# The last token tile of an SSD and attention layer written apart, its first tile's loads reordered, and merge weights asked for one unit earlier

## The chip, the core and the metric

The kernel runs on 1 core of a Trainium2 chip. TensorE (PE) multiplies, VectorE (DVE), ScalarE (ACT) and GpSimd (POOL) do the elementwise work, SyncE (SP) and ScalarE issue the DMAs. The metric is the device time of one execution in microseconds, the median of a few runs.

## The reference, cut to what matters

```python
h = rms_norm(x, norm_gain)                       # x: (1, 1024 tokens, 1024), all float32
q, k, v, z_a, z_s, xbc, dt_raw, gate_pre = split(h @ w_in)
branch_a = (window_attention(q, k, v, ...) * silu(z_a)) @ w_attn_proj
# SSD: causal conv + silu of xbc -> xs (32 heads of 64), B and C (4 groups of 128 states)
w = (C @ B.T) * decay * dt                       # inside a chunk
y = w @ xs + exp(a_cs) * (C @ prev_state) + d_skip * xs
state = state * chunk_decay + B.T @ (decay_to_end * dt * xs)   # handed to the next chunk
branch_b = rms_norm(y * silu(z_s), ssd_norm_gain) @ w_ssd_proj
merged = sigmoid(g_A) * branch_a + sigmoid(g_B) * branch_b
out = x + merged @ w_out
```

The state that a chunk leaves is read by the next chunk only. No one reads what the last one leaves.

## The kernel before, in words

Every float32 product is made exact enough by splitting both operands in a high and a low part and multiplying three of the four pairs, so each product of a weight unit (1024 x 128) with 512 tokens takes 24 matmuls of 128x512. ScalarE writes the high part of a weight unit (`high`, L189), GpSimd the low part (`low`, L192), and the raw unit comes by `load_w` (L199 to L205) into one of two slots; unit u may be loaded when the low part of unit u-2 is done. Unit u is multiplied when its low part is done.

The program has three blocks, one behind the other on each engine.

Block 1 (0 to 490 us) makes q, k, v, the conv channels and a part of z, and stores them to DRAM. Its last pair of units leaves `raw` in the tile `acc`, which is stored to `z_d`.

Block 2 (L1062 to L1488) walks over 8 tiles of 128 tokens in a loop. In each tile PE has eight halves of weight units to multiply (`half_unit(0)` to `half_unit(7)`, four units of gates and z), and between them the small products of attention and SSD: transposes (L1136), scores (L1129), attention times v (L1150), C times B (L1160), the inner part of y (`diag`, L1166), the part from the state (`off`, L1173) and the new state (`new_state`, L1179). SP loads a tile's operands in a fixed order in `tile_loads` (L1078): q, k, v, xb (16 rows of conv channels), then bc (B and C), a weight unit, `csb` (32 rows of cumulated decays, broadcast to 128 partitions: 2 MB), `zo`, `ecsb` (two broadcasts to 64 partitions each) and three more weight units. In the first tile bc goes ahead of the weight unit and of csb. csb, ecsb and yo (the output of the SSD) share the tile `acc` with what block 1 leaves there.

Block 3 has three passes of 8 weight units: the attention projection (unit 0 to 7, `unit3`, its operand o in X1), the first half of the SSD projection (8 to 15, operand in X0), the second half (16 to 23) with the merge, and then the output projection (24 to 31). Its units are called w0 to w31 here. Ahead of pass one the 8 tiles of o are loaded back from DRAM (L1552, L1554) and split, the first two tiles by DVE (L1713, L1716), six by ACT and DVE (L1661, L1716). PE's unit w2 needs `low` of w2, which GpSimd does after the squares of the first y tile (L1629, L1631). Those wait for ACT's sigmoid of the first gate tile (L1665) and the silu of the first y tile (L1653, L1703), and the loads of these wait on SP for the last stores of block 2. In the merge (L1729 to L1743) ACT does per unit the sigmoid of a gate, the high part of the merged half 0, `high` of the weight two units on, and the high part of half 1; DVE finishes a unit with the low part of half 1 (`m_lo`), and SP waits for that before it goes on to the next weight.

## Time and profile before

| | us |
|---|---|
| median of 3 runs (lowest, highest) | 1408.21 (1408.12, 1411.24) |
| the profiled execution | 1405.1 |
| its span | 1403.3 |
| PE busy in the span | 1356.0 |
| DVE, ACT, POOL busy | 794.6, 612.2, 586.9 |
| block 1, block 2, block 3 on PE | 0 to 490, 493 to 1026, 1026 to 1398 |

The span is what the trace covers; 1.8 us of the execution lie around it. The granted clock of PE is at its upper level in nearly the whole span (mean 0.99). Busy time alone doesn't show what is lost: the few places where PE stands still are read in its timeline, and what it waits for in the timelines of the other engines.

### The profile page before, as it was taken

What the parts mean: (1) busy time and instruction counts of PE and PEld (TensorE: products, weight loads), DVE (VectorE), ACT (ScalarE), POOL (GpSimd) and SP (SyncE); (2) the same over time, 40 slices, a digit from 0 to 9 for tenths busy, and PEclk for the clock granted to TensorE, in tenths of its full rate; (3) what the DMA queues carried; (4) which work ended last, traced back from release to release, by engine and by line L of the source; (5) the groups of instructions that cost most, each with busy time, mean ns of one, the idle gap of its engine ahead of it and who ended that gap; (6) DMA issues with size and microseconds to landing.
All of it is one profiled execution on the core that took longest, in us unless ns stands there. A gap on an engine that the chain in (4) does not pass through costs nothing.

```text
span 1403.3 us, 20569 instructions
## 1 busy us (share of the span) xinstructions
PE 1356.0 (97%) x7108; PEld 1085.9 (77%) x7108; DVE 794.6 (57%) x955; ACT 612.2 (44%) x1148; POOL 586.9 (42%) x344
## 2 busy tenths in 40 slices
PE   4999999999999989999999999999999999999999
PEld 4877777888888767778787878878768888777787
DVE  5876777766776344755565564646365554555311
ACT  5654435544455352525253545444356633323110
POOL 3634555544455342333333234243337666443321
PEclk9999999999999989999999999999999999999999
DMA  8333453433222475778777686767486265334421
GB/s 221 143 98 105 150 166 105 174 111 120 92 103 105 147 162 163 177 202 158 201 164 199 171 214 152 229 145 203 139 290 237 105 220 195 138 132 168 149 105 60
DMA packets 173669, 221.61 MB, mean 158 GB/s; under 512 B 7760, under 2 KB 136016, under 8 KB 173376
## 3 DMA queue, kind: packets, MB, share of 16 engines
q1 hardware_dynamic: 137808, 172.64, 43.3%
q10 hardware_dynamic: 35728, 48.37, 9.5%
q8 instruction: 19, 0.31, 0.1%
q14 instruction: 18, 0.15, 0.0%
q0 software_dynamic: 96, 0.13, 0.0%
HBM read 152.57 MB, written 63.31 MB: 154 GB/s over the span
## 4 chain that ended last, share of the span: by engine, by line
PE 79%; issue 9%; DVE 5%; DMA 3%; POOL 3%; ACT 2%; ACTq 0%; SPq 0%; POOLq 0%; DVEq 0%
PE F L180 34%; PE F L960 27%; PE F L1818 3%; PE M L1818 3%; PE M L1136 2%; PE M L1179 2%; DMA sb_early<-x_d 2%; POOL sb_res L1642 1%; PE F L1173 1%; PE F L1166 1%; PE F L1150 1%; PE M L1173 1%; PE M L1166 1%; PE F L1771 1%; DMA sb_early<-x 1%
## 5 line engine op out<-in xcount | busy, mean ns | idle before, releaser
L180 PE MATMUL F<-sb_xb,sb_whl 128*128 128x512 f32 x1536 | 376.7, 402 | 0.0
L180 PEld LDWEIGHTS F<-sb_xb,sb_whl 128*128 128x128 f32 x1536 | 287.1, 189 | 75.2 <-issue 8.8
L192 POOL TENSOR_TENSOR sb_whl<-sb_wst,sb_whl 128x1024 fp32r<-128x1024 f32 x64 | 160.7, 2511 | 403.6 <-ACT sb_whl L189 403.1
L180 PE MATMUL F<-sb_X,sb_whl 128*128 128x512 f32 x1104 | 259.5, 396 | 3.6 <-POOL sb_whl L192 2.6
L180 PEld LDWEIGHTS F<-sb_X,sb_whl 128*128 128x128 f32 x1104 | 206.6, 187 | 56.0 <-issue 5.5
L960 PE MATMUL F<-sb_tv,sb_whl 128*128 128x512 f32 x1008 | 243.5, 397 | 2.3 <-DVE sb_acc L761 2.3
L960 PEld LDWEIGHTS F<-sb_tv,sb_whl 128*128 128x128 f32 x1008 | 190.0, 189 | 49.4 <-issue 2.7
L415 POOL TENSOR_TENSOR sb_whl<-sb_acc,sb_whl 128x512 fp32r<-128x512 f32 x103 | 146.1, 1426 | 137.6 <-ACT sb_whl L472 137.6
L960 PE MATMUL F<-sb_xb,sb_whl 128*128 128x512 f32 x756 | 186.4, 399 | 1.8 <-DVE sb_part L751 1.8
L960 PEld LDWEIGHTS F<-sb_xb,sb_whl 128*128 128x128 f32 x756 | 142.2, 189 | 40.3 <-issue 5.0
L189 ACT ACTIVATE sb_whl<-sb_wst 128x1024 fp32r<-128x1024 f32 x64 | 67.6, 1057 | 208.3 <-DMA sb_wst<-w_units 108.3
L1406 ACT ACTIVATE sb_res<-F 128x512 f32<-128x512 f32 x64 | 38.3, 598 | 182.0 <-PE F L180 182.0
L807 DVE SCALAR_TENSOR_TENSOR M<-sb_acc,M 128x1023 f32<-128x1023 f32 (+2 forms) x72 | 92.4, 1284 | 15.7 <-ACT M L574 14.8
L472 ACT ACTIVATE sb_whl<-sb_acc 128x512 fp32r<-128x512 f32 x103 | 63.7, 627 | 73.0 <-PE F L960 61.6
L415 POOL TENSOR_TENSOR sb_whl<-sb_wst,sb_whl 128x512 fp32r<-128x512 f32 x44 | 63.9, 1454 | 75.4 <-ACT sb_whl L472 75.3
L1397 ACT ACTIVATE sb_early<-sb_acc,sb_ncs_sb 128x128 f32<-128x128 f32 x256 | 77.4, 394 | 7.5 <-DVE sb_acc L1292 7.5
L1301 DVE TENSOR_TENSOR sb_early<-sb_early 128x1024 f32<-128x1024 f32 x32 | 45.9, 1454 | 55.5 <-ACT sb_early L1397 55.5
L1706 DVE SCALAR_TENSOR_TENSOR sb_X<-sb_X,sb_cst x16 | 54.6, 3411 | 35.9 <-POOL sb_part L1629 35.9
L1306 DVE TENSOR_TENSOR sb_acc<-sb_acc,M 128x512 f32<-128x512 f32 x16 | 11.0, 688 | 79.6 <-PE M L1173 72.8
L1465 POOL TENSOR_TENSOR sb_early<-sb_early,sb_ssd_sb 128x512 f32<-128x512 f32 x32 | 32.8, 1046 | 49.5 <-DVE sb_early L1276 49.5
L1703 DVE TENSOR_TENSOR sb_X<-sb_X x16 | 23.0, 1441 | 51.4 <-ACT sb_X L1653 51.4
L1629 POOL TENSOR_TENSOR sb_part<-sb_X 128x1024 f32 x16 | 30.3, 1896 | 46.0 <-DVE sb_X L1703 46.0
(223 smaller groups left out, 1780.3 us busy)
## 6 DMA issues: line engine op xcount, KB each, us to landing
sb_wst<-w_units SPq DMA_DIRECT2D x64, 512.0 KB, 6.1
sb_acc<-cs_d SPq DMA_DIRECT2D x8, 2048.0 KB, 21.6
sb_wst<-w_units SPq DMA_DIRECT2D x12, 1024.0 KB, 4.9
x_d<-sb_res ACTq DMA_DIRECT2D x24, 512.0 KB, 2.6
sb_acc<-w_units SPq DMA_DIRECT2D x10, 1024.0 KB, 5.0
sb_early<-x_d SPq DMA_DIRECT2D x8, 1024.0 KB, 9.1
sb_acc<-ecs_d SPq DMA_DIRECT2D x16, 512.0 KB, 23.4
z_d<-sb_res ACTq DMA_DIRECT2D x16, 512.0 KB, 6.6
```

The lines of the kernel that those rows point to most:

```text
L180: last = nc.tensor.matmul(bank, weight(slot, wp, k), act(ap, k, half), start=(k == 0 and wp == 0 and ap == 0), stop=(k == NK - 1 and wp == 1))
L189: return nc.scalar.activation(weights(slot, 0), raw_unit(slot), ACT.Copy)
L192: return nc.gpsimd.tensor_tensor(weights(slot, 1), raw_unit(slot), weights(slot, 0).bitcast(f32), ALU.subtract)
L415: nc.gpsimd.tensor_tensor(ring(idx, 1), operand(n, order(n)[idx]), ring(idx, 0).bitcast(f32), ALU.subtract).then_inc(p_lo, 1)
L472: nc.scalar.activation(ring(idx, 0), operand(n, order(n)[idx]), ACT.Copy).then_inc(p_hi, 1)
L807: ins = nc.vector.scalar_tensor_tensor(to[:, back:], raw[:, u, 0:T - back], tap(2 * m + u, 3 - back), to[:, back:], ALU.mult, ALU.add)
L960: last = nc.tensor.matmul(F[:, BANK[what], :], ring(idx, wp)[:, k * P:(k + 1) * P], moving(what, ap, k), start=(idx < 4 and k == 0 and wp ...
L1301: nc.vector.tensor_tensor(dec[:, g % 2], dec[:, g % 2], cbm[:, g, :].unsqueeze(1).to_broadcast([P, HG, P]), ALU.mult).then_inc(wT_ready, 1)
L1397: last = nc.scalar.activation(dec[:, g % 2, h, :], csb[:, HG * g + h, :], ACT.Exp, bias=ncs_sb[:, ds(j, 1), HG * g + h:HG * g + h + 1].rea ...
L1406: nc.scalar.activation(res[:, p, (h % 2) * HALF:(h % 2 + 1) * HALF], F2[:, h % 2, :], ACT.Copy).then_inc(half_taken, 1)
L1706: nc.vector.scalar_tensor_tensor(split_tile(X, 1, i, s), y, C("ssd_gain", q0, q0 + 8)[:, ds(i * 2 + s, 1)], tile(X, 0, i, s), ALU.mult, AL ...
L1818: last = nc.tensor.matmul(row_bank(t), X0[:, ap, k, t * P:(t + 1) * P], w_half[wp][:, (k % 2) * HALF:(k % 2 + 1) * HALF], start=(k == 0 an ...
```

## The change

Five things, which go together in the text of the program:

- Block 2's loop runs over 7 tiles, and the last tile is written apart, without the transposes of B, the products and sums of the new state, the decay of the old state and their waits.
- In that last tile ACT takes the high parts of all eight o tiles as soon as PE is done with `off(3)`, ahead of `take_half(7)` and `unit_out(3)`; POOL makes the low parts of o tiles 3 and 5, DVE those of the other six. DVE makes no high parts any more. The store of y is issued before the last unit is taken, not after.
- First tile: SP issues q, k, v, xb first, then w0 and w1 of this block, then csb, bc and the next weight unit. The waits for the stores of `z_d` move from ahead of csb to ahead of zo, and GpSimd waits for them before its loop.
- In the tile `acc` csb moves to the upper end, so that ecsb and yo lie over `raw`.
- Merge: w18 and w19 are asked for ahead of the loop, and in the loop w(20 + 2i + s) is asked for where w(19 + 2i + s) was, ahead of the load of the residual rows.

```diff
+    def loop_and_last(self, eng_loop, count, steps):
+        for i in self.loop(eng_loop, count - 1, steps):
+            yield i, False
+        yield count - 1, True
...
-            sp.wait_ge(p_lo, 7 * NPAIR)
-            load_w(sp, 0, 0, 0)
-            load_w(sp, 1, 0, 0)
...
-        csb, w = carve(acc_all, 0, NHS, P)
-        ecsb, w = carve(acc_all, w, 16, P)
+        ecsb, w = carve(acc_all, 0, 16, P)
         yo, w = carve(acc_all, w, 16, P)
+        csb, w = carve(acc_all, w, NHS, P)
...
+        O_POOL = (3, 5)
+        O_DVE = NK - len(O_POOL)
...
                 if first:
+                    sp.wait_ge(p_lo, 7 * NPAIR)
+                    load_w(sp, 0, 0, 0)
+                    load_w(sp, 1, 0, 0)
+                    load_decays(j, at_j)
                     sp.wait_ge(prod, 7 * (NPAIR - 1) + 5)
                     load_bc(j, at_j)
-                load_w(sp, B2 + 2, 4, j)
-                sp.wait_ge(dec_ready, j * 4 + 1)
+                    load_w(sp, B2 + 2, 4, j)
+                else:
+                    load_w(sp, B2 + 2, 4, j)
+                    load_decays(j, at_j)
+                    load_bc(j, at_j)
+                sp.wait_ge(o_stored, j * 16 + 16)
                 if first:
                     for p in range(2):
                         sp.wait_ge(z_stored[p], 16 * 4)
-                sp.dma_start(csb[:], cs_d[:, ds(at_j, P)].partition_broadcast(P)).then_inc(cs_in, 16)
-                if not first:
-                    load_bc(j, at_j)
-                sp.wait_ge(o_stored, j * 16 + 16)
...
-                new_state(0)
-                new_state(1)
+                if not last_tile:
+                    pe.wait_ge(brow_ready, at(1, 1))
+                    new_state(0)
+                    new_state(1)
...
                 take_half(6)
-                take_half(7)
-                unit_out(3)
+                if last_tile:
+                    act.wait_ge(yg_done, 4 * NT + 1)
+                    for k in range(NK):
+                        act.wait_ge(o_in[k], 16)
+                        nc.scalar.activation(X1[:, 0, k, :], X1[:, 1, k, :].bitcast(f32), ACT.Copy).then_inc(o_hi, 1)
+                else:
+                    take_half(7)
+                    unit_out(3)
                 act.wait_ge(yout_ready, at(4, 5))
                 act.dma_start(y_d[:, :, ds(j * P, P)].rearrange("n p t -> p n t"), yo[:]).then_inc(y_stored, 16)
+                if last_tile:
+                    take_half(7)
+                    unit_out(3)
...
+                if last_tile:
+                    for k in O_POOL:
+                        pool.wait_ge(o_hi, k + 1)
+                        nc.gpsimd.tensor_tensor(X1[:, 1, k, :], X1[:, 1, k, :].bitcast(f32), X1[:, 0, k, :].bitcast(f32),
+                                                ALU.subtract).then_inc(o_lo, 1)
...
+            load_w(sp, B3 + 18, 0, 0)
+            load_w(sp, B3 + 19, 0, 0)
             with nc.sync.Fori(0, 3) as i:
                 for s in range(2):
-                    load_w(sp, B3 + 18 + s, 2, i)
                     sp.wait_ge(m_lo, i * 4 + (2 * s + 2))
                     load_merge(i + 1, s)
+                    load_w(sp, B3 + 20 + s, 2, i)
                     load_rows(i, s)
-            for s in range(2):
-                load_w(sp, B3 + 24 + s, 0, 0)
...
             for k in range(NK):
-                if k < DVE_TILES:
-                    dve.wait_ge(o_in[k], 16)
-                    ch.link(nc.vector.tensor_copy(X1[:, 0, k, :], X1[:, 1, k, :].bitcast(f32)))
-                else:
-                    dve.wait_ge(act_hi, k - DVE_TILES + 1)
-                nc.vector.tensor_tensor(X1[:, 1, k, :], X1[:, 1, k, :].bitcast(f32), X1[:, 0, k, :].bitcast(f32),
-                                        ALU.subtract).then_inc(act_lo, 1)
+                if k not in O_POOL:
+                    dve.wait_ge(o_hi, k + 1)
+                    nc.vector.tensor_tensor(X1[:, 1, k, :], X1[:, 1, k, :].bitcast(f32), X1[:, 0, k, :].bitcast(f32),
+                                            ALU.subtract).then_inc(act_lo, 1)
```

SP's issues at the start of block 2, first tile, before. `sb_early<-x_d` with 16 rows is xb, with 8 rows bc; `sb_acc<-cs_d` is csb, `sb_acc<-ecs_d` ecsb, `sb_wst<-w_units` a weight unit.

```order
L205 DMA sb_wst<-w_units 128x1024
L1062 UNCONDITIONAL_BRANCH
L1080 DMA sb_early<-q_d 128x8x128
L1081 DMA sb_early<-k_d 128x2x192
L1084 DMA sb_early<-v_d 128x256
L1087 DMA sb_early<-x_d 128x16x128
L1076 DMA sb_early<-x_d 128x8x128
L205 DMA sb_wst<-w_units 128x1024
L1096 DMA sb_acc<-cs_d 128x32x128
L1100 DMA sb_early<-z_d 128x8x128
L1103 DMA sb_acc<-ecs_d 64x16x128
```

The same piece now:

```order
L1077 UNCONDITIONAL_BRANCH
L1099 DMA sb_early<-q_d 128x8x128
L1100 DMA sb_early<-k_d 128x2x192
L1103 DMA sb_early<-v_d 128x256
L1106 DMA sb_early<-x_d 128x16x128
L211 DMA sb_wst<-w_units 128x1024
L1091 DMA sb_acc<-cs_d 128x32x128
L1095 DMA sb_early<-x_d 128x8x128
L1123 DMA sb_early<-z_d 128x8x128
L1126 DMA sb_acc<-ecs_d 64x16x128
```

The first two weight units moved behind xb, and csb moved ahead of bc (a weight unit still stands between bc and z_d).

PE at the end of the last tile, before: the last halves of units (L180), diag (L1166), off (L1173), new_state (L1179), and the first product of block 3 (L1771).

```order
L1166 MATMUL M<-sb_early 64x128 x8
L1173 MATMUL F<-sb_early,sb_part 128x128 x4
L1173 MATMUL M<-sb_early,sb_part 128x128 x4
L1179 MATMUL M<-sb_early 128x512 x2
L180 MATMUL F<-sb_xb,sb_whl 128x512 x24
L1755 UNCONDITIONAL_BRANCH
L1771 MATMUL F<-sb_X,sb_whl 128x512 x24
```

And now:

```order
L1190 MATMUL M<-sb_early 64x128 x8
L1197 MATMUL F<-sb_early,sb_part 128x128 x4
L1197 MATMUL M<-sb_early,sb_part 128x128 x4
L186 MATMUL F<-sb_xb,sb_whl 128x512 x24
L1792 UNCONDITIONAL_BRANCH
L1811 MATMUL F<-sb_X,sb_whl 128x512 x24
```

`new_state` is gone between off and the last half of a unit.

## Rows read from the trace of the kernel before

**Rows 1.** The page, part 4: the chain that ended last, shares by engine

```profile
PE 79%; issue 9%; DVE 5%; DMA 3%; POOL 3%; ACT 2%; ACTq 0%; SPq 0%; POOLq 0%; DVEq 0%
```

**Rows 2.** Chain of waits, first pass of block 3: start us, us, what

```profile
1038.25 84.00 PE F L180 x360
```

**Rows 3.** Timeline of PE, merge: start us, us, line, operands, xcount [idle <-releaser]

```profile
1213.00 45.36 PE L180 MATMUL F<-sb_X,sb_whl 128*128 128x512 f32 x192
1259.86 23.02 PE L180 MATMUL F<-sb_X,sb_whl 128*128 128x512 f32 x96 [1.50 <-POOL sb_whl L192]
...
1315.83 5.85 PE L1818 MATMUL F<-sb_whl,sb_X 128*128 128x512 f32 x24 [0.90 <-DVEq L1736]
```

**Rows 4.** Timelines of SP and ACT, merge: a weight's load and high part

```profile
1249.67 0.33 SPq L205 DMA_DIRECT2D sb_wst<-w_units  x1
...
1256.10 1.06 ACT L189 ACTIVATE sb_whl<-sb_wst 128x1024 fp32r<-128x1024 f32 x1 [4.01 <-DMA sb_wst<-w_units]
```

**Rows 5.** Timelines of POOL and DVE, merge: two instructions at one time

```profile
1228.89 2.41 POOL L192 TENSOR_TENSOR sb_whl<-sb_wst,sb_whl 128x1024 fp32r<-128x1024 f32 x1 [3.36 <-ACT sb_whl L189]
...
1229.47 2.38 DVE L1738 TENSOR_TENSOR sb_acc<-sb_acc,sb_res 128x512 f32 x1
```

**Rows 6.** Timeline of PE, last tile and first product of block 3

```profile
1018.77 1.88 PE L1179 MATMUL M<-sb_early 128*128 128x512 f32 x4
1020.09 6.15 PE L180 MATMUL F<-sb_xb,sb_whl 128*128 128x512 f32 x24
...
1031.40 6.85 PE L1771 MATMUL F<-sb_X,sb_whl 128*128 128x512 f32 x18 [2.80 <-DVE sb_X L1716]
```

**Rows 7.** Timelines of SP, ACT, DVE and POOL from the last tile into block 3

```profile
1014.83 3.36 SPq L1552 DMA_DIRECT2D sb_X<-o_d  x7
1023.88 0.34 SPq L1554 DMA_DIRECT2D sb_X<-o_d  x1
...
1027.56 0.48 ACTq L1449 DMA_DIRECT2D y_d<-sb_acc  x1
1028.58 5.79 ACT L1661 ACTIVATE sb_X<-sb_X 128x1024 fp32r<-128x1024 f32 x6 [0.75 <-issue]
1038.54 1.28 ACT L1665 ACT_TABLE_LOAD   x1 [4.17 <-DMA sb_acc<-g_d]
...
1029.67 7.36 DVE L1716 TENSOR_TENSOR sb_X<-sb_X 128x1024 fp32r<-128x1024 f32 x6 [2.08 <-ACT sb_X L1661]
...
1049.65 3.19 POOL L192 TENSOR_TENSOR sb_whl<-sb_wst,sb_whl 128x1024 fp32r<-128x1024 f32 x1 [0.16 <-POOL sb_ssd_sb L1631]
```

**Rows 8.** L1554's instruction, landing times

```profile
DMA to landing us min/median/max: 3.7/3.7/3.7
```

**Rows 9.** Timeline of PE, first tile of block 2

```profile
493.15 1.18 PE L1136 MATMUL M<-sb_cst,sb_early 128*128 128x128 f32 x8 [3.52 <-issue]
...
508.96 1.47 PE L1136 MATMUL M<-sb_cst,sb_early 128*128 128x128 f32 x12
...
522.38 1.97 PE L1136 MATMUL M<-sb_cst,sb_early 128*128 128x128 f32 x8 [4.44 <-DVE sb_early L1287]
524.00 7.70 PE L180 MATMUL F<-sb_xb,sb_whl 128*128 128x512 f32 x24
```

**Rows 10.** Windows of 4 us: PE, PEld, DVE, ACT, POOL busy, PEclk, DMA share, GB/s

```profile
524.00:528.00 4.00, 4.00 (x12) 3.14 (x11) 0.84 (x2) 3.12 (x10) 0.00 (x0) 0.50 0.48 36
```

**Rows 11.** Timelines of SP, DVE and ACT, first and second tile

```profile
484.64 0.38 SPq L1087 DMA_DIRECT2D sb_early<-x_d  x1
...
552.69 0.38 SPq L1087 DMA_DIRECT2D sb_early<-x_d  x1
...
518.32 2.36 DVE L1292 TENSOR_TENSOR sb_acc<-sb_acc,sb_ssd_sb 128x1024 f32<-128x1024 f32 x2 [10.84 <-DMA sb_acc<-cs_d]
...
546.00 1.06 ACT L189 ACTIVATE sb_whl<-sb_wst 128x1024 fp32r<-128x1024 f32 x1 [13.67 <-DMA sb_wst<-w_units]
```

**Rows 12.** Chain of waits, second tile: the load of bc

```profile
561.65 22.83 DMA sb_early<-x_d
```

More of the change, by code:

```diff
@@ L1059, in build, with tiles @@
             "q_in", "k_in", "x2_in", "v_in", "bc_in", "cs_in", "ecs_in", "z_in", "o_stored", "y_stored")
+        def tiles(loop):
+            with loop(0, NT - 1) as j:
+                yield j, False
+            yield NT - 1, True
+        o_in = sems(*[f"o_in{k}" for k in range(NK)])
+        o_hi, o_lo = sems("o_hi", "o_lo")
+        O_POOL = (3, 5)
+        O_DVE = NK - len(O_POOL)
         @block.sync
@@ L1117, in _ @@
             pe.wait_ge(b12_moved, 32)
-            with nc.tensor.Fori(0, NT) as j:
+            for j, last_tile in tiles(nc.tensor.Fori):
                 def at(n, k):
@@ L1237, in _ @@
                 off(3)
-                pe.wait_ge(state_ready, at(4, 3))
-                new_state(2)
-                new_state(3)
+                if not last_tile:
+                    pe.wait_ge(state_ready, at(4, 3))
+                    new_state(2)
+                    new_state(3)
                 half_unit(7)
@@ L1248, in _ @@
             ch.link(nc.vector.tensor_scalar(stat[:, 5, :], C("sinks"), -1.0, None, ALU.mult))
-            for j in ch.loop(nc.vector.Fori, NT, 4 * 3 + 2 * 2):
+            for j, last_tile in ch.loop_and_last(nc.vector.Fori, NT, 4 * 3 + 2 * 2):
                 def at(n, k):
@@ L1350, in _ @@
                 y_take(0)
-                add_state(0)
-                add_state(1)
+                if not last_tile:
+                    add_state(0)
+                    add_state(1)
                 weights_T(2)
@@ L1371, in _ @@
             act.wait_ge(ncs_ready, 1)
-            with nc.scalar.Fori(0, NT) as j:
+            for j, last_tile in tiles(nc.scalar.Fori):
                 def at(n, k):
@@ L1425, in _ @@
                 probs_out(1)
-                act.wait_ge(brt_done, at(1, 1))
-                nc.scalar.activation(flat(brow[:]), S[:, 0, :], ACT.Copy).then_inc(brow_ready, 1)
+                if not last_tile:
+                    act.wait_ge(brt_done, at(1, 1))
+                    nc.scalar.activation(flat(brow[:]), S[:, 0, :], ACT.Copy).then_inc(brow_ready, 1)
                 unit_out(0)
@@ L1455, in _ @@
             pool.wait_ge(state_zero, 1)
-            with nc.gpsimd.Fori(0, NT) as j:
+            for p in range(2):
+                pool.wait_ge(z_stored[p], 16 * 4)
+            for j, last_tile in tiles(nc.gpsimd.Fori):
                 def at(n, k):
@@ L1499, in build @@
             "ms_done", "ms_rt", "rms_ready", "acc_ready", "m_hi", "m_lo", "rows_in", "row_done", "out_ready", "out_stored")
-        o_in = sems(*[f"o_in{k}" for k in range(NK)])
         gateA_in = sems("gateA_in0", "gateA_in1")
@@ L1656, in silu_and_high @@
                                      scale=C("ssd_gain", q0, q0 + 8)[:, ds(i * 2 + s, 1)]).then_inc(act_hi, 1)
-            act.wait_ge(st_done, 4 * NT)
-            for k in range(DVE_TILES, NK):
-                act.wait_ge(o_in[k], 16)
-                nc.scalar.activation(X1[:, 0, k, :], X1[:, 1, k, :].bitcast(f32), ACT.Copy).then_inc(act_hi, 1)
             with nc.scalar.Fori(0, 4) as i:
@@ L1768, in unit3 @@
                         for k in range(NK):
-                            pe.wait_ge(act_lo, tiles + k + 1)
+                            if tiles == 0 and k in O_POOL:
+                                pe.wait_ge(o_lo, O_POOL.index(k) + 1)
+                            else:
+                                pe.wait_ge(act_lo, tiles + k + 1 - (0 if tiles else sum(q < k for q in O_POOL)))
                             for wp, ap in ((0, 0), (0, 1), (1, 0)):
@@ L1783, in _ @@
                     unit3(2 + s, X1, i)
-            unit3(8, X0, 0, tiles=8)
+            unit3(8, X0, 0, tiles=O_DVE)
             unit3(9, X0, 0)
```

45 lines of the change are left out of this document (25 added, 20 removed).

## The prediction, made before the changed kernel was run

> **What bounds the kernel now.** I read the page first. Its chain of waits lies on PE for 79% of the span, and what it calls issue is mostly time around PE's small steps [rows 1]. So an edit pays only where PE stands still, or where it takes work off PE. The next view is PE's timeline, which marks each stretch of matmuls and the idle time ahead of it. PE is late in three places: in the first tile of block 2, between block 2 and block 3, and in the merge. The change touches all three. The timelines of the other engines, read backwards from each idle time, tell what was late. A matmul of 128x512 costs 84.00 / 360 = 0.2333 us when nothing waits [rows 2]: 24 of them 5.60 us, a unit of 48 11.20 us.
>
> **The merge: -7.5 us.** Units 16 to 23 are 384 matmuls, and 24 of the output projection follow before the last stretch shown. From 1213.00 to 1315.83 are 102.83 us, and 408 x 0.2333 is 95.2, so 7.6 us are lost, with the slow first matmul of the last stretch 7.9 [rows 3]. The releaser of the first wait is GpSimd's low part of a weight. Its high part on ACT waited 4.01 us for the DMA, which was asked for at 1249.67 and had landed by 1256.10, 6.4 us later [rows 4]. The loop closes on itself: SP asks for a weight only behind the wait for `m_lo` of the unit before, ACT stands in that wait with the high part of half 1 queued behind it, and that high part gives the next `m_lo`. The period of this loop is longer than PE's 11.2 us, so PE meets it from the third unit on.
>
> Now w20 is asked for when w19 was, one unit of 11.2 us further on. The load of 6.4 us is hidden by PE's own unit, and `high` of a weight then waits for PE to be done with the slot two units back, which leaves 11.2 - 1.06 - 2.41 = 7.7 us of slack for the two splits [rows 4, 5]. The x rows go behind the weight on SP's queue. They are needed in the output projection alone. w19 itself waits for the low part of w17 and stands ahead of the second merge load only by that, long before PE needs it. Nothing else in the loop has a period of more than a unit as far as I see. Bounds: 2.4 (the 1.50 and the 0.90 that the shown rows mark as waits, were another chain almost as long) to 7.9. I take 7.5, near the upper end, because the slack is so large.
>
> **The last tile and the start of block 3: -2.5 us.** Off PE go two stretches of `new_state`, each 1.88 us as shown and 1.7 without the overlap at its end, and 4 of the 12 transposes of a row of 1.47, or 0.5 [rows 6, 9]. Together that is 3.9 us. The last `half_unit` started at 1020.7 and ended at 1026.3; now it should end at 1022.4. The first product with o ended at 1038.25, which is where the long stretch begins [rows 2]. So PE took 12.0 us for 5.6 us of work: it waited for the low parts of o (2.80 in the last wait), and 18 matmuls took 6.85 us in place of 4.2 [rows 6].
>
> Who makes the parts now: the loads of o start when the store of o lands, 1014.83 before, now 2.2 earlier (one new_state and the transposes are gone ahead of it), 1012.6. DVE is free of y when the load of the last o tile is issued, 1023.88 before. That moves by the same 2.2 and by two state sums less on DVE, about 1.3, to 1020.4, and the tile lands 3.7 us later, 1024.1 [rows 7, 8]. ACT's copies cost 5.79 / 6 = 0.97 each and can start when `off(3)` is done, 1016.8; the eighth ends near 1025.5. DVE's low parts cost 7.36 / 6 = 1.23 each from 1020.4 on, GpSimd's two 2.4 each. If they run side by side, the first product ends near 1029.5, 8.8 earlier than before.
>
> What is late next: unit w2. PE would ask for it one half and one unit after that, 1029.5 + 16.8 = 1046.3. Its low part ended at 1052.84, and PE asked at 1038.25 + 16.8 = 1055.05. The chain to this low part starts at the store of y: issued 1027.56, the first gate tile lands and ACT starts on it at 1038.54, and another 14.3 us of table load, sigmoid, silu, product, squares and low part end at 1052.84 [rows 7]. None of it is shortened by the change. The store of y now stands directly behind the eighth copy, so it is issued near 1026 in place of 1027.56, and the store of the last unit goes behind it, which holds SP's wait for both. So w2 is ready near 1051.3. PE then stands still for about 5 us. A pause like that has a second price: after 4.44 us of idle time in the first tile PE's granted clock was 0.50 for 4 us (1.2 GHz in place of 2.4), and the next 24 matmuls took 7.70 in place of 5.60, 2.1 more [rows 9, 10]. Gain: 1055.05 - 1051.3 - 2.1 = 1.7. If the pause is shorter because the low parts of o come later, PE's pauses are the same ones in another place. The old pauses had the same price, though, and I give back part of it: 2.5. Bounds: -1 (w2 ready 1 us earlier only, and a clock price of 2.1) to 8.8 (w2 is no limit).
>
> VectorE and GpSimd beside each other are a doubt of its own. While GpSimd ran a low part from 1228.89 to 1231.30, a sum of 128x512 on DVE that had started at 1229.47 ended at 1231.85, after it [rows 5]. So the two seem not to run their two-input instructions at once. In the change six DVE and two GpSimd subtractions stand for PE together: 6 x 1.23 + 2 x 2.4 = 12.2 us from 1020.4 on if in turn, so the first product ends near 1033.3 and PE asks for w2 at 1050.1. That is just under 1051.3, so the gain changes by little. The Trainium skill, "SBUF — State Buffer", Terms, says the port pair of VectorE and GpSimd is locked for a whole instruction and the loser blocks. By that rule giving tiles 3 and 5 to GpSimd gains nothing over leaving them on DVE (12.2 against 8 x 1.23 = 9.8); the row agrees with the lock.
>
> **The first tile: 0 us.** Before, csb landed at 518.3 and DVE had waited 10.84 us for it; PE lost 4.44 us and the clock's 2.1 [rows 9, 11]. Now csb is asked for some 11 us earlier, behind xb and two weights. But bc is behind csb now, and PE needs bc at its transposes, which were reached at 508.96 [rows 9]. The second tile has the same order of loads: xb was issued at 552.69 and bc landed at 561.65 + 22.83 = 584.48, 31.8 us later [rows 11, 12]. From 484.64, with one weight more in front, that gives 516.5 to 518. PE would reach the transposes near 507.7, as xb lands 1 to 2 us sooner without the 1 MB of weights ahead of it. So PE waits 9 to 10 us there, and pays the clock's 2.1, where it had waited 4.44 and 2.1 later on and 3.52 ahead of its first matmul, of which it saves 1.3. csb then no longer costs it anything. Balance: +9.5 - 4.4 - 1.3 = +3.8 at that place. Behind it PE had to wait anyway: the fourth weight unit landed at 546.0, behind all of the tile's loads, and the decays, the state and `diag(2)` hung on it [rows 11]. The sum of the bytes ahead of it is the same, the two weights at the front start 2 us later, and 1 us of a hole ahead of csb closes. This end moves by less than 2 us either way, and it swallows most of the 3.8. I take 0. Bounds: -2 (bc lands at 513, the rest follows it) to +5 (bc at 520 and the PE bound).
>
> Moved at no cost: GpSimd's wait for `z_d` stands ahead of a loop whose first instruction waits for DVE anyway. The new place of csb holds no other reader. The tiles 1 to 6 have the same instructions in the same order. More instructions are fetched, since the last tile is written apart; no wait for code of more than a us shows at the block changes.
>
> **Sum.** 0 - 2.5 - 7.5 = -10.0 us on the profiled execution: span 1393.3, execution 1395.1. The median of the runs stands 3.1 us above the profiled execution, so 1408.2 - 10.0 = 1398.2.
>
> **The rivals.**
> - A. The start of block 3 is free (8.8 in place of 2.5). For it: the chain to w2 has 2.2 us of slack now, and y is stored earlier. Against: its 25 us don't get shorter. 1391.9. Chance 0.10.
> - B. bc holds the first tile in full and the clock price stays: first tile +5, start of block 3 nearer to its lower end, 0. 1408.2 + 5 - 7.5 = 1405.7. For it: the second tile's loads. Against: the weight at 546.0 gives room. Chance 0.12.
> - C. The merge doesn't get what it says: another step of its loop (the merge loads behind `m_lo`, GpSimd's product) is as long, and only 2.4 come. 1403.3. Against: the wait named is the DMA's. Chance 0.08.
> - D. Slower than before: csb's descriptors, started among the xb and z traffic, go at a much lower rate, and bc with them. It decides if bc lands later than about 529: then the first tile costs over 12 us, more than the rest gains. At 535 (18 us behind the forecast's 517) it is 1398.2 + 18 = 1416. Against: the second tile had the same mixture and took 31.8 us. Chance 0.04.
> - The forecast has 0.66.
>
> **How the numbers follow.** A run of this kernel can be told from no change from about 0.3%, 4.2 us. Faster (below 1404.0): the forecast, A, and most of C, with a rest of the forecast's own spread taken off, 0.84. Same: B and the near ends, 0.11. Slower: D and a corner of B, 0.05. The range reaches to A on one side and past C on the other: 1391 to 1404. The forecast's own range is 1394 to 1402.
>
> **What would show it.** In the merge ACT's high parts wait for no DMA, and PE runs from unit 16 into the output projection with no idle time over 0.5 us; the stretch is about 95 us. At the start of block 3 the first product ends 4 to 9 us after the last `half_unit`'s 5.6, and PE has a new idle time ahead of w2, with GpSimd's low part as its releaser and the clock at its lower level behind it. In the first tile PE's idle time ahead of L1136 at 522 is gone, and one of 7 to 10 us ahead of the transposes of bc, released by the DMA, is there. I am wrong if PE waits for the merge's weights still, if w2 shows no wait, or if bc lands before 512 or after 522.

## The result, and the profile after

| | before | changed |
|---|---|---|
| median, us (lowest, highest; runs) | 1408.62 (1408.12, 1411.24; 4) | 1394.70 (1390.57, 1399.94; 4) |
| the profiled execution, its span | 1405.1, 1403.3 | 1399.9, 1398.1 |

The ratio is 0.990 (95% interval 0.986 to 0.994), 13.9 us between the medians where 10.0 were forecast. The four runs lie 9.4 us apart, and the profiled one is the slowest of them, so its span is only 5.2 us shorter than before's. It shows what each part did, but not how much is given back on average. For that the experiments below leave twelve more profiles.

**The first tile.** PE's timeline; names and columns as in [rows 9], `transpose` is L1159 now and a unit's half L186:

```profile
489.30 1.09 PE L1159 MATMUL M<-sb_cst,sb_early 128*128 128x128 f32 x8
...
494.77 11.46 PE L186 MATMUL F<-sb_xb,sb_whl 128*128 128x512 f32 x48 [2.47 <-POOL sb_whl L198]
...
507.39 0.65 PE L1159 MATMUL M<-sb_cst,sb_early 128*128 128x128 f32 x4 [0.28 <-DMA sb_early<-x_d]
...
515.48 1.09 PE L1159 MATMUL M<-sb_cst,sb_early 128*128 128x128 f32 x8
516.33 5.83 PE L186 MATMUL F<-sb_xb,sb_whl 128*128 128x512 f32 x24
```

The wait of 4.44 us and the slow 24 matmuls behind it are gone, and PE waits 0.28 us for bc where 9 to 10 were expected. The tile starts 3.9 us earlier, and the second one (its first scores) at 558.81 in place of 569.59: 10.8 us, where 0 was forecast. SP's timeline shows how; `x_d` is xb and then bc, `cs_d` is csb:

```profile
475.33 0.37 SPq L1099 DMA_DIRECT2D sb_early<-q_d  x1
...
477.43 0.38 SPq L1106 DMA_DIRECT2D sb_early<-x_d  x1
480.10 1.45 SPq L211 DMA_DIRECT2D sb_wst<-w_units  x2
481.59 0.43 SPq L1091 DMA_DIRECT2D sb_acc<-cs_d  x1
483.60 10.98 SPq L1095 DMA_DIRECT2D sb_early<-x_d  x1
494.68 5.38 SPq L211 DMA_DIRECT2D sb_wst<-w_units  x1
505.30 0.37 SPq L1123 DMA_DIRECT2D sb_early<-z_d  x1
```

And the same of before, with SP's longest wait there:

```profile
482.37 0.38 SPq L1080 DMA_DIRECT2D sb_early<-q_d  x1
...
485.12 4.34 SPq L1076 DMA_DIRECT2D sb_early<-x_d  x1
495.06 0.34 SPq L205 DMA_DIRECT2D sb_wst<-w_units  x1
497.05 0.39 SPq L1096 DMA_DIRECT2D sb_acc<-cs_d  x1
```

```profile
SPq L205 <- POOL sb_whl L415: 36.8, 1, 36.8
```

The reader is to see two things. xb was issued at 484.64 [rows 11] only because it stood behind w0, and w0 waits for GpSimd's last low part of block 1; now it goes at 477.43. And csb went at 497.05, behind the third weight (495.06) and the end of z_d's stores; now it goes at 481.59, 15.5 us earlier, while the last two stores of z_d are still to be issued (487.99 and 490.59); over its old room it could not. The fourth weight lands 10.8 us earlier with them, 535.2 for 546.0.

**Given back.** In the profiled run the later tiles lose 8.3 of the 10.8 us: the last one starts at 959.32 where it was 961.84. Three of PE's waits in block 2:

```profile
575.98 1.11 PE L1159 MATMUL M<-sb_cst,sb_early 128*128 128x128 f32 x4 [2.93 <-DMA sb_early<-x_d]
...
578.45 7.43 PE L186 MATMUL F<-sb_xb,sb_whl 128*128 128x512 f32 x24
...
841.72 0.65 PE L1159 MATMUL M<-sb_cst,sb_early 128*128 128x128 f32 x4 [1.64 <-DMA sb_early<-x_d]
...
908.12 0.65 PE L1159 MATMUL M<-sb_cst,sb_early 128*128 128x128 f32 x4 [0.96 <-DMA sb_early<-x_d]
```

These are waits for bc, 5.5 us in all, which lands 22.6 us after its issue in the median and 25.0 at most (before 21.4 and 22.8). Behind the first of them PE also runs slowly, 7.43 us for 24 matmuls. This is the most that any profile gives back; the mean over all of them is 0.7 us, as the paragraph on all profiles below says. In the chain of waits DMA has 9% in place of 3% [rows 1]:

```profile
PE 76%; DMA 9%; issue 6%; DVE 4%; POOL 3%; ACT 2%; SPq 0%; ACTq 0%; POOLq 0%; DVEq 0%
```

**The last tile and block 3.** PE, answering to [rows 6]:

```profile
1014.15 5.84 PE L186 MATMUL F<-sb_xb,sb_whl 128*128 128x512 f32 x24
...
1027.74 2.93 PE L1811 MATMUL F<-sb_X,sb_whl 128*128 128x512 f32 x6 [0.71 <-POOL sb_X L1531]
1032.13 1.65 PE L1811 MATMUL F<-sb_X,sb_whl 128*128 128x512 f32 x3 [1.47 <-DVE sb_X L1753]
1033.58 18.02 PE L186 MATMUL F<-sb_X,sb_whl 128*128 128x512 f32 x72
1052.65 67.45 PE L186 MATMUL F<-sb_X,sb_whl 128*128 128x512 f32 x288 [1.05 <-POOL sb_whl L198]
```

The new wait ahead of w2 is there, behind GpSimd's low part, but it is 1.05 us long, where the forecast had 5 or, with the low parts in turn, 1.2, and the clock does not fall behind it (288 matmuls in 67.45 us, 0.234 each). w2 starts 2.4 us earlier than before (1055.05), and block 2 had already brought 2.5: the part itself gave nothing in this run. ACT shows why. Its first copy of an o tile, here and in a second run of almost the same kernel (E12 below):

```profile
1016.34 1.06 ACT L1479 ACTIVATE sb_X<-sb_X 128x1024 fp32r<-128x1024 f32 x1 [5.19 <-DMA sb_X<-o_d]
```

```profile
1008.88 2.17 ACT L1479 ACTIVATE sb_X<-sb_X 128x1024 fp32r<-128x1024 f32 x2 [3.28 <-PE M L1197]
```

Counted from the start of the last tile, E12's copy starts at 55.0 us, released by `off(3)` as the forecast has it. This one starts at 57.0, released by the load of o. The store of y stands behind the copies, so here it is issued 66.7 us into the tile, later than before (65.7), and in E12 at 64.1. DVE and GpSimd beside each other, the low parts of o:

```profile
1023.24 2.22 DVE L1753 TENSOR_TENSOR sb_X<-sb_X 128x1024 fp32r<-128x1024 f32 x1 [1.33 <-ACT sb_X L1479]
1025.79 6.29 DVE L1753 TENSOR_TENSOR sb_X<-sb_X 128x1024 fp32r<-128x1024 f32 x2 [0.33 <-ACT sb_X L1479]
```

```profile
1024.55 3.13 POOL L1531 TENSOR_TENSOR sb_X<-sb_X 128x1024 fp32r<-128x1024 f32 x1 [0.18 <-ACT sb_X L1479]
1028.54 2.46 POOL L198 TENSOR_TENSOR sb_whl<-sb_wst,sb_whl 128x1024 fp32r<-128x1024 f32 x1 [0.85 <-ACT sb_whl L195]
```

Two subtractions that take 1.23 us each alone took 6.29 together beside two instructions of GpSimd.

**The merge.** PE, answering to [rows 3]:

```profile
1210.85 90.16 PE L186 MATMUL F<-sb_X,sb_whl 128*128 128x512 f32 x384
1301.31 5.86 PE L1858 MATMUL M<-sb_whl,sb_X 128*128 128x512 f32 x24 [0.30 <-issue]
1310.67 5.85 PE L1858 MATMUL F<-sb_whl,sb_X 128*128 128x512 f32 x24 [3.51 <-DVEq L1773]
```

The units run through without a wait, as forecast, and then PE stands 3.51 us ahead of the second part of the output projection. It waits there for a pair of PSUM banks that DVE has not taken yet: the merge on ACT, GpSimd and DVE is behind. From the first of these starts to the one after the last shown (1316.36) are 105.5 us, before 108.5: 3.0 gained, not 7.5.

### The profile page after: what moved, and what is told of

It reads as the page before. It is cut to its first block, busy times and chain, and to the rows that moved or that the text cites. A ratio compares the mean times of both kernels' runs of the same rounds, so it can differ in the third digit from the quotient of the medians.

```text
span 1398.1 us, 20354 instructions
## 1 busy us (share of the span) xinstructions
PE 1353.0 (97%) x7096; PEld 1082.6 (77%) x7096; DVE 810.9 (58%) x947; ACT 613.4 (44%) x1148; POOL 582.4 (42%) x338
## 4 chain that ended last, share of the span: by engine, by line
PE 76%; DMA 9%; issue 6%; DVE 4%; POOL 3%; ACT 2%; SPq 0%; ACTq 0%; POOLq 0%; DVEq 0%
PE F L186 32%; PE F L963 27%; DMA sb_early<-x_d 7%; PE F L1858 3%; PE M L1858 3%; PE M L1159 2%; POOL sb_res L1687 1%; PE M L1203 1%; PE F L1197 1%; PE F L1190 1%; PE F L1173 1%; PE M L1197 1%; PE M L1190 1%; POOL sb_whl L198 1%; DMA sb_early<-x 1%
## 5 line engine op out<-in xcount | busy, mean ns | idle before, releaser
L186 PE MATMUL F<-sb_xb,sb_whl 128*128 128x512 f32 x1536 | 376.1, 402 | 2.5 <-POOL sb_whl L198 2.5
L186 PEld LDWEIGHTS F<-sb_xb,sb_whl 128*128 128x128 f32 x1536 | 286.6, 188 | 77.0 <-issue 10.4
L186 PE MATMUL F<-sb_X,sb_whl 128*128 128x512 f32 x1104 | 259.8, 397 | 1.1 <-POOL sb_whl L198 1.1
L186 PEld LDWEIGHTS F<-sb_X,sb_whl 128*128 128x128 f32 x1104 | 207.8, 188 | 52.8 <-issue 1.7
L963 PEld LDWEIGHTS F<-sb_xb,sb_whl 128*128 128x128 f32 x756 | 142.3, 189 | 40.3 <-issue 5.0
L418 POOL TENSOR_TENSOR sb_whl<-sb_wst,sb_whl 128x512 fp32r<-128x512 f32 x44 | 64.1, 1458 | 75.6 <-ACT sb_whl L475 75.6
L1327 DVE TENSOR_TENSOR sb_early<-sb_early 128x1024 f32<-128x1024 f32 x32 | 56.8, 1794 | 52.4 <-ACT sb_early L1425 52.3
L1858 PE MATMUL F<-sb_whl,sb_X 128*128 128x512 f32 x192 | 46.2, 396 | 3.5 <-DVEq L1773 3.5
L1505 POOL TENSOR_TENSOR sb_early<-sb_early,sb_ssd_sb 128x512 f32<-128x512 f32 x28 | 29.6, 1079 | 45.0 <-DVE sb_early L1302 38.0
```

The costliest lines, as they stand in the source:

```text
L186: last = nc.tensor.matmul(bank, weight(slot, wp, k), act(ap, k, half), start=(k == 0 and wp == 0 and ap == 0), stop=(k == NK - 1 and wp == 1))
L418: nc.gpsimd.tensor_tensor(ring(idx, 1), operand(n, order(n)[idx]), ring(idx, 0).bitcast(f32), ALU.subtract).then_inc(p_lo, 1)
L963: last = nc.tensor.matmul(F[:, BANK[what], :], ring(idx, wp)[:, k * P:(k + 1) * P], moving(what, ap, k), start=(idx < 4 and k == 0 and wp ...
L1327: nc.vector.tensor_tensor(dec[:, g % 2], dec[:, g % 2], cbm[:, g, :].unsqueeze(1).to_broadcast([P, HG, P]), ALU.mult).then_inc(wT_ready, 1)
L1858: last = nc.tensor.matmul(row_bank(t), X0[:, ap, k, t * P:(t + 1) * P], w_half[wp][:, (k % 2) * HALF:(k % 2 + 1) * HALF], start=(k == 0 an ...
```

## The experiments

All compare with the kernel before on the same chip. "Merge stretch" is PE's time from the start of unit 16 to the third part of the output projection (before 108.5); "second tile" and "last tile" are the starts of their scores (before 569.6 and 961.8); "boundary" is from the last tile's start to unit 16 (before 251.2).

**E1. The changed kernel once more.** No edit.

> The changed kernel once more, to have a second profile and its spread. Theory T: the first tile gains about 10.8 us (PE's second tile starts near 559 where before started at 569.6), and bc, which waits behind csb, gives back an amount that differs from run to run: the profiled run above, 1399.9, gave back 8.3 us by the last tile, so a run near 1392 should give back almost nothing. Median 1391 to 1398, the runs 5 us or more apart, and in the new profile the waits of PE for bc (DMA from x_d) are fewer or shorter when its time is lower. Rival R: the spread lies elsewhere (the start of block 3 or the merge), and the last tile of block 2 starts 2.5 us earlier than before in any run.

1391.88 us (1390.94 to 1395.54, 6 runs, so 4.6 us apart where 5 or more were expected), ratio 0.990 (0.988 to 0.992). The profile is of a run of 1390.98: second tile 558.9, last tile 951.7, so of 10.7 us 10.1 are still there; PE waits 0.8 us for bc in all tiles together, against 5.8 in the run of 1399.94. T holds in the main: of the 9 us between these two runs 7.6 stand there at the last tile, and 2.6 more come between it and unit 16. The merge stretch was 106.7.

**E2. The merge alone.** On the kernel before:

```diff
+            load_w(sp, B3 + 18, 0, 0)
+            load_w(sp, B3 + 19, 0, 0)
             with nc.sync.Fori(0, 3) as i:
                 for s in range(2):
-                    load_w(sp, B3 + 18 + s, 2, i)
                     sp.wait_ge(m_lo, i * 4 + (2 * s + 2))
                     load_merge(i + 1, s)
+                    load_w(sp, B3 + 20 + s, 2, i)
                     load_rows(i, s)
-            for s in range(2):
-                load_w(sp, B3 + 24 + s, 0, 0)
```

> The kernel before with the merge's weights asked for one unit further on, and nothing else. Theory T: 3.0 us off before, as the two profiles show from 1213 to the output projection (105.5 in place of 108.5 us); PE's idle time ahead of the output projection grows from 0.90 to about 3.5, since another chain of the merge loop (ACT's sigmoid, GpSimd's product, DVE's sums) has a period of about 12.0 us against PE's 11.2. Rival R, the prediction's: 7.5 us, the wait of 3.5 being an accident of one run.

1403.42 us (12 runs) against 1406.87, ratio 0.998 (0.996 to 0.999): 3.2 us (1.3 to 5.2). Merge stretch 106.95, and the wait of 3.47 us is back, with a slow x24 behind it (7.41). T holds, the 7.5 does not. Beside the kernel before's own 108.5 the stretch shows 1.6 us, beside the mean of all profiles of the old form (109.5) 2.6.

**E3. The first tile alone.** The order of the loads, csb at the upper end of `acc` and GpSimd's earlier wait, on the kernel before (these pieces of the diff ahead of the prediction, no others).

> The kernel before with the first tile's loads, the room of csb and GpSimd's earlier wait for z_d changed, and nothing else. Theory T: the second tile starts 10 to 11 us earlier; later tiles give back between 0 and 8 of it at the waits for bc, so the time is 2.5 to 10.8 us under before and its runs are further apart than before's. Rival R, the prediction's: 0 us (between -2 and +5).

1395.68 us (6 runs), ratio 0.992 (0.990 to 0.994): 11.0 us (8.3 to 13.8), just above the upper end of T. Second tile 558.8, last tile 952.3. This one part brings three quarters of the whole, and the forecast gave it nothing. Its runs (1394.6 to 1399.3) are not further apart than before's (1402.0 to 1411.1 in 23), so that half of T's expectation is not shown.

**E4. The last tile alone.** Written apart on the kernel before, with the copies and subtractions of o moved as in the change.

> The kernel before with the last tile written apart, and nothing else. Theory T: 0 to 1 us off before, since unit w2 of block 3 hangs on the store of y and the first gate tile and starts 2.4 us earlier only because all of block 2 did; PE waits about 1 to 4 us ahead of w2. Rival R, the prediction's: 2.5 us. Rival A: 8.8 us (w2 is no limit).

1405.49 us (12 runs), ratio 0.9991 (0.9977 to 1.0006): 1.3 us, between 3.2 gained and 0.8 lost. Boundary 248.3. Neither T nor the 2.5 can be excluded by it, A can. The boundary alone is 2.9 us shorter than before's, but the merge stretch was 110.1.

**E8. bc ahead of csb in the first tile**, on the changed kernel:

```diff
-                    load_decays(j, at_j)
                     sp.wait_ge(prod, 7 * (NPAIR - 1) + 5)
                     load_bc(j, at_j)
+                    load_decays(j, at_j)
```

> The changed kernel with bc ahead of csb in the first tile again; q, k, v and xb stay ahead of w0 and w1, and csb's room stays. Theory T: the early start of q to xb (they no longer stand behind the wait for the low part of block 1's last weight) makes most of the first tile's 10.8 us, csb lands a few us later than now, and the second tile starts 7 to 11 us earlier than in the kernel before. Rival R: csb ahead of bc makes the gain, and without it the second tile starts less than 4 us earlier than before.

1393.34 us (6 runs), ratio 0.991 (0.990 to 0.993), second tile 558.2: the order of these two makes no difference. csb was issued at 482.75, ahead of the third weight still, and landed as early, not a few us later as T has it. The second tile is T's number, but T's reason is not the right one, as the next run shows.

**E11. q, k, v and xb ahead of w0 and w1, and nothing else**, on the kernel before:

```diff
-            sp.wait_ge(p_lo, 7 * NPAIR)
-            load_w(sp, 0, 0, 0)
-            load_w(sp, 1, 0, 0)
...
                 if first:
+                    sp.wait_ge(p_lo, 7 * NPAIR)
+                    load_w(sp, 0, 0, 0)
+                    load_w(sp, 1, 0, 0)
                     sp.wait_ge(prod, 7 * (NPAIR - 1) + 5)
                     load_bc(j, at_j)
                 load_w(sp, B2 + 2, 4, j)
```

> The kernel before with q, k, v and xb of the first tile issued ahead of w0 and w1, and nothing else: csb keeps its room over what block 1 stores to z_d, its wait for that store and its place behind bc. Theory T: the first scores of block 2 start 2 to 4 us earlier, but csb is issued at about the same time as before (497), so PE waits for it the longer, the second tile starts 0 to 3 us earlier and the time is 0 to 3 us under before. It is then csb's new room that makes the other 7 us. Rival R: the order alone makes most of it, 7 us or more.

1406.92 us (12 runs), ratio 0.9995 (0.9983 to 1.0007). The first scores start at 490.4, 3.8 us earlier, but the second tile at 568.0, 1.6 us earlier than in the profile of before, as T has it. Its SP and DVE rows (`cs_d` on DVE is the first reader of csb):

```profile
494.71 0.33 SPq L205 DMA_DIRECT2D sb_wst<-w_units  x1
495.14 0.40 SPq L1096 DMA_DIRECT2D sb_acc<-cs_d  x1
```

```profile
516.06 3.12 DVE L1292 TENSOR_TENSOR sb_acc<-sb_acc,sb_ssd_sb 128x1024 f32<-128x1024 f32 x2 [9.73 <-DMA sb_acc<-cs_d]
```

With csb at 495.14 its reader starts at 516.06; in the changed kernel, with csb at 481.59, at 505.75, and in E8 at 505.41. So the gain of the first tile is csb going out ahead of the third weight. In E11 SP did not wait for the stores of z_d any more, the third weight alone held csb. The new room is needed all the same: the last store over the old one was issued at 490.71 only. No run has csb ahead of the third weight over its old room, so the two aren't measured apart. The earlier q to xb alone is worth nothing measurable. Windows of 24 us, columns as in [rows 10], of before, of E11 and of the changed kernel:

```profile
476.00:500.00 24.00, 20.48 (x141) 16.64 (x140) 6.51 (x17) 6.89 (x10) 9.01 (x5) 0.93 0.76 226
```

```profile
476.00:500.00 24.00, 21.41 (x144) 16.97 (x144) 10.81 (x18) 7.71 (x15) 9.02 (x5) 0.93 0.76 234
```

```profile
476.00:500.00 24.00, 21.40 (x151) 17.08 (x150) 10.80 (x18) 7.81 (x15) 9.00 (x5) 1.00 0.95 222
```

The DMA engines were busy for 0.76 of this time before. In E11 they start 4 us sooner and stand idle later (0.49 and 0.37 in the two windows of 4 us from 488 on), 0.76 again. With csb in that place they are busy for 0.95.

**E5. bc on ACT's queue** in tiles 1 to 7 of the changed kernel:

```diff
                     load_w(sp, B2 + 2, 4, j)
                     load_decays(j, at_j)
-                    load_bc(j, at_j)
...
                 else:
+                    act.wait_ge(yg_done, at(4, 5))
+                    act.dma_start(bc[:], x_d[16:24, :, ds(j * P + P, P)].rearrange("n p t -> p n t")).then_inc(bc_in, 16)
                     take_half(7)
```

> The changed kernel with bc of tiles 1 to 7 issued on ACT's queue, right behind the store of y, instead of on SP's behind csb. Theory T: what is given back after the first tile comes from bc waiting behind csb, so PE's waits for the DMA from x_d ahead of C times B go, the gain of 10.8 us at the second tile is still there at the last, and the time is 2 to 6 us under the changed kernel's with its runs closer together (within 3 us). Rival R: the give-back is csb or the weights being late as well, or the clock; then the waits only change their name, and the time is the changed kernel's within 1 us.

1395.07 us (6 runs, 1394.0 to 1399.2), ratio 0.993 (0.991 to 0.994): not faster than the changed kernel (E1's ratio is 0.990), and the runs are 5.2 us apart, not 3. E8 on the same chip took 1.7 us less, so R's "within 1 us" is not shown either. PE waits for bc no more, but the waits have changed their name, as R has it:

```profile
678.51 1.09 PE L1189 MATMUL F<-sb_early 128*64 128x128 f32 x16 [1.10 <-DVE sb_early L1326]
...
744.62 1.09 PE L1189 MATMUL F<-sb_early 128*64 128x128 f32 x16 [0.54 <-DVE sb_early L1326]
```

```profile
665.16 0.69 DVE L1331 TENSOR_TENSOR sb_acc<-sb_acc,M 128x512 f32<-128x512 f32 x1 [5.59 <-DMA sb_acc<-ecs_d]
```

In that tile DVE, which PE now waits for, had itself stood 5.59 us for ecsb, another load of SP's queue. The second tile started at 558.5 and the last one at 953.8: of 11.1 us 8.0 are left, so with bc out of the way PE still lost 3.1 us here. In E7 below, where bc's loads are the same, it lost nothing (559.7 and 951.7). T's cure is not shown to do anything, and what is lost differs from run to run with it too.

**E6 and E12. ACT's merge loop written out**, on the changed kernel; the same kernel on two chips:

```diff
-            with nc.scalar.Fori(0, 4) as i:
+            for i in range(4):
                 for s in range(2):
                     act.wait_ge(merge_in[s], i * 32 + 32)
```

> The changed kernel with ACT's merge loop written out instead of a loop of four, which takes away the reload of its function table at the head of each round (1.28 us in every second unit). Theory T: the merge's other chain through ACT goes from 12.0 to about 11.4 us a unit, PE's wait of 3.51 ahead of the output projection falls to 1 or less, and the time is 2 to 3 us under the changed kernel's. Rival R: the chain is held by DVE and GpSimd blocking one another (sums of 2.38 in place of 0.69 us) or by the merge loads; then the wait stays at 3 to 3.5 and the time is the same within 1 us.

> The changed kernel with ACT's merge loop written out, once more, as the measure for the runs beside it: 1386 to 1390.

1388.26 us (4 runs), ratio 0.987 (0.985 to 0.988), and 1391.19 us (4 runs), ratio 0.989 (0.987 to 0.991). The second missed its range by 1.2 us, beside a before of 1407.57. Merge stretch 101.2 in both, 5.4 us under the mean of the changed form: 432 matmuls at 0.2333 us are 100.8, so nothing is left in it. That is more than T's 2 to 3 us; R falls. ACT, changed kernel, two units of the merge, and then E6's:

```profile
1278.53 0.63 ACT L1722 ACTIVATE sb_X<-sb_acc  x1 [3.88 <-DVE sb_acc L1777]
...
1289.78 0.63 ACT L1722 ACTIVATE sb_X<-sb_acc  x1 [3.90 <-DVE sb_acc L1777]
1290.43 1.28 ACT L1727 ACT_TABLE_LOAD   x1
1291.73 1.15 ACT L1727 ACTIVATE sb_res<-sb_res,sb_cst 128x1024 f32<-128x1024 f32 x1
...
1302.52 0.63 ACT L1722 ACTIVATE sb_X<-sb_acc  x1 [3.89 <-DVE sb_acc L1777]
```

```profile
1269.14 0.63 ACT L1722 ACTIVATE sb_X<-sb_acc 128x512 fp32r<-128x512 f32 x1 [3.79 <-DVE sb_acc L1777]
...
1280.17 0.63 ACT L1722 ACTIVATE sb_X<-sb_acc 128x512 fp32r<-128x512 f32 x1 [3.80 <-DVE sb_acc L1777]
1280.71 1.14 ACT L1727 ACTIVATE sb_res<-sb_res,sb_cst 128x1024 f32<-128x1024 f32 x1
...
1291.29 0.63 ACT L1722 ACTIVATE sb_X<-sb_acc 128x512 fp32r<-128x512 f32 x1 [3.79 <-DVE sb_acc L1777]
```

1278.53 to 1302.52 are 24.0 us for two units, 12.0 each, against PE's 11.2. E6's 1269.14 to 1291.29 are 22.15, 11.07 each, just under PE. The loop's head loads ACT's table anew in every second unit, and that stands in a chain in which every step waits for the one before: sigmoid (ACT), product (GpSimd, 2.41), sum (DVE), high part and weight (ACT), low part of the weight (GpSimd, 2.40), sum (DVE), high part (ACT). By the Trainium skill, "ScalarE activation tables: per-element evaluation and per-set limits", Table sets in the compiler and the runtime, the table loads are placed per block. The trace agrees: each of the loop's four rounds begins with one, and the loop written out shows one ahead of its first unit and none behind it.

**E9. The same loop as two rounds of four units**, a table load in every fourth:

```diff
-            with nc.scalar.Fori(0, 4) as i:
-                for s in range(2):
+            with nc.scalar.Fori(0, 2) as ii:
+                for q in range(2):
+                    i = ii * 2 + q
+                    for s in range(2):
```

> The changed kernel with ACT's merge loop as two rounds of four units, so that its function table is loaded in every fourth unit instead of every second. Theory T (a chain through ACT, GpSimd and DVE of 24.0 us in two units with one load of the table in it, 22.15 without): four units take 46.1 us, 11.54 a unit, so the chain slips 0.34 us a unit behind PE's 11.20 instead of 0.8, and PE's wait ahead of the second row of the output projection falls from 3.5 to between 0 and 1.5; the merge stretch is 102 to 104 us, 1387.5 to 1390 in all. Rival R: it is the loop as such and not what stands in the chain; the wait stays near 3.5.

```profile
1300.68 5.85 PE L1860 MATMUL F<-sb_whl,sb_X 128*128 128x512 f32 x24 [1.08 <-DVEq L1775]
```

The wait is 1.08 and the stretch 102.5, between 101.2 and 106.7 as T has it. Halving the rounds halves the loads and all else that a round's head costs, so this run alone doesn't tell the two apart. The spacing of ACT's copies does: in this run two units take 23.95 us with the load among them and 22.54 without, 1.41 more, of which the load is 1.28. Why 22.54 is still 0.4 us over the 22.14 of the loop written out stays open. The total, 1393.88 us (6 runs), ratio 0.990 (0.988 to 0.992), is outside T's range: the runs scatter from 1389.9 to 1396.1, and such a total can't resolve the 2 to 4 us that the profile shows.

**E7. Both, bc on ACT's queue and the merge loop written out.**

> The two edits before this one together: bc on ACT's queue and ACT's merge loop written out. Theory T: the sum of the two, 4 to 8 us under the changed kernel. Rival R: no more than the larger of the two.

1387.13 us (4 runs), ratio 0.987 (0.985 to 0.989), the merge stretch 101.2. By the ratios it is 3.7 us under the changed kernel (E1), and E6 is 4.1 under it: that is R, no more than E6 alone.

**E10. E12 without the last tile written apart.**

> The changed kernel with ACT's merge loop written out and the last tile left in the loop as before: the first tile's loads and the merge alone. Theory T: the last tile written apart is worth about 1 us, so this takes 0 to 2 us more than the same kernel with it (run again beside it). Rival R, the prediction's size: 2.5 us or more.

1391.25 us (4 runs), ratio 0.989 (0.987 to 0.991), beside E12's 1391.19. The part is worth nothing that this measurement can tell; each of the two is known to about 3 us, so R isn't excluded. In the two profiles the boundary is 251.0 in E10 and 248.5 in E12.

**All profiles together.** The boundary was 249.98 us in the mean of the nine profiles with the last tile written apart (248.3 to 253.1) and 250.94 to 251.16 in the five without: 1.0 us. The nine fall in two groups. In E1, E4, E6 and E12 the loads of o go out by 51.1 us after the start of the last tile, ACT's first copy starts at 55.0 behind `off(3)`, w2 is ready at 89.9 to 90.5, and the boundary is 2.0 to 2.7 us shorter. In the other five the loads go out at 52.1 to 53.7, the first copy waits for them, w2 is ready at 91.5 to 93.1 (before 91.0), and the boundary is between 1.0 shorter and 2.1 longer. In four of these five ACT had taken a weight of that tile late as well (40.3 to 41.9 in place of 37.9 to 39.0), which delays the store of o behind it; in the fifth, E8, only the store's landing was late. The second tile started at 559.2 in the mean of the ten with the new first tile (557.3 to 561.6) and at 566.6 to 569.6 in the three without any of it, mean 568.4: 9.2. From the second to the last tile it was 394.3 in the mean of these ten (392.0 to 400.5) and 393.6 in the four with the old room of csb (392.3 to 394.9): 0.7 us given back on average. The merge stretch was 108.5 to 110.6 in four of the old form, 105.5 to 107.0 in five of the new one: 2.9. The three parts measured alone, 11.0 + 3.2 + 1.3 = 15.5 us, agree with the whole of E1, 14.6 (11.8 to 17.4).

## Why the forecast was right, and by which of its steps it was not

1398.2 forecast, 1394.7 measured, within the range and on the right side. Its terms were 0, -2.5 and -7.5; the runs say about -9 to -11, -1 and -3. Two large errors of opposite sign met, and the total is right by luck.

- **The first tile: the step that failed** is "From 484.64, with one weight more in front, that gives 516.5 to 518", and behind it "The sum of the bytes ahead of it is the same". The step took xb's issue time of before as fixed, although the change moves it past a wait of SP (36.8 us in the list of waits, never looked at for what it held back), and it let csb start 11 us earlier for csb's sake only. Here the 2 MB went out 15.5 us earlier, and all that follows them came earlier: bc landed near 507, not 517, and the fourth weight, which was to swallow every gain, 10.8 us earlier. The forecast counted 1 us of a hole, where the DMA engines' share over 24 us rose from 0.76 to 0.95. E11 shows that the move of xb is not what paid; csb ahead of the third weight is. The second tile's 31.8 us was a fair measure: in the changed kernel xb to bc took 30.0 us, only from 477.43 and not from 484.64.
- **Rival B** (bc holds the first tile) is refuted with a wait of 0.28 us. Its mechanism exists, though: in later tiles bc holds PE, and in the profiled run this cost 5.5 us of waits, most of the 8.3 given back. D did not occur.
- **The merge: the mechanism was right, and the size was off.** ACT waits for no weight any more and PE runs 384 matmuls without a stop. But "Nothing else in the loop has a period of more than a unit as far as I see" was wrong: the chain with the table load has 12.0 us. It came close to the bounds' lower end, 2.4, and is rival C, which had 0.08. E6, E9 and E12 show it: with a table load in every second unit, in every fourth and in the first alone the stretch is about 106.6, 102.5 and 101.2 us. The table load was to be seen in the trace of before, 1.28 us in every second unit.
- **The last tile.** The new wait ahead of w2 with GpSimd's low part as its releaser came as forecast, and so did the doubt on VectorE and GpSimd. The first product ended 2.0 us earlier than before once block 2's 2.5 are taken off, where 8.8 or, in turn, 5 was forecast. w2 was ready at 1052.4 + 2.5 = 1054.9 on before's scale, not at 1051.3, because the store of y came 0.9 us later into the tile and not 1.5 earlier: the step "the loads of o start when the store of o lands ... 1012.6" held in four profiles of nine, and they gain the 2.0 to 2.7 us of the forecast; in the other five o was late. The forecast's clock price behind that wait did not come; in this run it was paid ahead of w2, 18.02 us for 72 matmuls in place of 16.8. By the Trainium skill, "SBUF — State Buffer", Terms, the port pair is locked for a whole instruction and the loser blocks. The trace agrees: two subtractions in 6.29 us in place of 2.46 beside GpSimd, the second ending at 1032.08, 1.08 us after GpSimd's second instruction.
- **The range** held the time although two of three terms lay outside or at the edge of their own bounds (first tile -2 to +5). Errors that cancel are no merit of the working.

What stays open: why the same kernel gives back 8.3 us in one run and 0.7 in another, and why o and the weight ahead of it come late in five profiles of nine. The waits name the tile's loads, and in E5 moving one of them only names another, but nothing here shows what makes them slower in one run. That ecsb takes bc's place in E5 is read from one tile's rows and was not tried by itself.

E6 and E7 have the lowest times of all; between them the runs can't tell. That they beat the changed kernel is clear from the merge stretch, less so from the totals: E12, the same kernel as E6, has 0.989 beside E1's 0.990.

## What to carry to other kernels

When a load is moved to the front of a queue, work out anew the issue time of everything behind it, from the list of what the queue waits for: where a big transfer stands behind a wait, look at the DMA engines' share in that stretch. If they are idle there, as in E11, sending it earlier brings everything behind it forward. When one wait in a loop is removed, add up the period of every other chain through the same loop, instruction by instruction, before its gain is put at the full distance to the bound; a table load at a loop's head counts. And forecast a sum by its terms' bounds: the total can be right when the terms are not.

## What the runs showed of the hardware that was not expected

- The same pause costs PE's clock in one run and not in another. Behind 2.47 us of idle time in the first tile, which follow 3 us of small matmuls, 48 matmuls took 11.46 us in the changed kernel's profile and 13.01 in E12's. Of eleven profiles with this pause seven have 11.44 to 11.46 us and four 12.88 to 13.01 (E6, E7, E11, E12). Windows of 4 us, columns as in [rows 10], of the changed kernel and of E12:

```profile
495.00:499.00 4.00, 4.00 (x18) 3.22 (x18) 3.76 (x7) 2.00 (x4) 3.61 (x2) 1.00 1.04 143
```

```profile
495.00:499.00 4.00, 4.00 (x13) 3.12 (x14) 3.76 (x7) 1.90 (x4) 3.70 (x2) 0.66 1.04 115
```

  The granted clock was 1.00 in the one, the level of 2.4 GHz, and 0.66 in the other, a mean of that level and 1.2 GHz. Ahead of the output projection 3.51 us of idle time were followed by 5.85 us for 24 matmuls, and 3.47 to 3.49 in E1, E2, E5 and E8 by 7.20 to 7.41. By the Trainium skill, "TensorE: Matmul & The Clock Gate", Part 1, how many matmuls run slowly at a kernel's start differs from run to run of the same kernel. These rows show the like behind a pause in the middle of a kernel, about 1.5 us each time, which is part of the scatter between runs.
- SP stood 10.98 us in the issue of bc behind csb (483.60), and 0.38 us in the same issue when csb was behind it (E8, 482.33). The issue that stood right behind csb was the long one each time, whatever it loaded: 13.23 us for zo in the kernel before, 12.77 in E11.
